# Two transformer blocks on one core: a table load and a weight split moved at the first block's attentions, decays' middles moved under a projection, and norms turned through two PSUM pools

## The reference, cut to what matters

```python
def first_block(x, ...):                       # 2 layers
    for i in range(2):
        h = rms_norm(x, ln_attn_g[i])
        dq, dk, dv, mq, mk, mv = split(h @ w_in[i])       # 6 x 512 columns
        # each head of dq, dk, mq, mk is rms-normed over its 64 columns
        y_diff = softmax(dq dk + bias)[0] - lam * softmax(...)[1]  @ dv, rms-normed per head
        y_moba = softmax(mq mk + bias) @ mv
        x = x + concat(y_diff, y_moba) @ w_out[i]
        x = x + conv_ffn(rms_norm(x, ln_ffn_g[i]), w_up[i], conv_w[i], conv_b[i], w_down[i])

def second_block(h_lat, ctx, ...):             # 2 layers, latent and context stream
    modulate = lambda h, gain, shift, scale: rms_norm(h, gain) * (1 + scale) + shift
    # layer 0: an RWKV-7 scan in both directions over 8 heads, whose decays are
    #   w = exp(-exp(-softplus(-w_raw) - 0.5)), and a windowed attention of 8 heads with a sink
    # layer 1: a neighbourhood attention and a global attention, latent stream alone
    h = h + gate * rms_norm(mixer(modulate(h)) @ w_out)     # both streams in layer 0
    f = square(relu(modulate(h) @ w_ff1)) @ w_ff2
    h = h + gate * rms_norm(f)
```

## Time and profile before

| | us |
|---|---|
| median of 3 runs | 2012.1 (2010.51 to 2012.96) |
| the profiled execution, its own time | 2011.27 |
| its span in the profile | 2009.2 |
| PE busy in the span | 1901.4 (95%) |
| DVE busy | 1122.7 (56%) |
| ACT busy | 867.5 (43%) |
| POOL busy | 211.4 (11%) |

### The profile page before, as it was taken

The page is one execution under the profiler, slowest core; times in us unless marked ns, Lnnn a source line. Parts: engine busy times, 40 slices in busy tenths (PEclk is TensorE's granted clock), DMA queues, the critical chain, the costliest instruction groups (busy, mean ns, idle before and its releaser), DMA issues. The chain is left out here.

```text
span 2009.2 us, 36599 instructions
## 1 busy us (share of the span) xinstructions
PE 1901.4 (95%) x15600; PEld 1591.5 (79%) x15600; DVE 1122.7 (56%) x1758; ACT 867.5 (43%) x1559; POOL 211.4 (11%) x249
## 2 busy tenths in 40 slices
PE   7989999998999999989999998999999989988998
PEld 5758998775899888756898987888877787678987
DVE  6655774565566564475557665544444646436643
ACT  5465663445456542455322335322232344545532
POOL 1100221110022100102112211000000101000000
PEclk9989999998999999999999998999999999988999
DMA  7666665466666542343000042333332224024653
GB/s 266 232 228 210 189 189 169 167 230 210 208 170 187 180 138 62 111 152 122 25 4 4 3 148 63 117 95 112 98 99 90 84 66 145 1 64 128 187 189 126
DMA packets 219352, 264.52 MB, mean 132 GB/s; under 512 B 14214, under 2 KB 153782, under 8 KB 214711
## 3 DMA queue, kind: packets, MB, share of 16 engines
q1 hardware_dynamic: 218603, 261.36, 40.8%
q10 hardware_dynamic: 588, 0.82, 0.1%
HBM read 261.07 MB, written 1.09 MB: 130 GB/s over the span
## 5 line engine op out<-in xcount | busy, mean ns | idle before, releaser
L403 PE MATMUL acc<-rounded,rounded 128*128 128x512 f32 (+1 forms) x2552 | 880.3, 345 | 27.8 <-DVE rounded L675 12.9
L404 PE MATMUL acc<-rounded,rounded 128*128 128x512 f32 (+1 forms) x2552 | 871.2, 341 | 0.0
L405 PE MATMUL acc<-rounded,rounded 128*128 128x512 f32 (+1 forms) x2552 | 870.8, 341 | 0.0
L387 DVE TENSOR_TENSOR rounded<-arena,rounded 128x2048 fp32r<-128x2048 f32 (+1 forms) x194 | 434.4, 2242 | 298.7 <-ACT rounded L376 298.6
L403 PEld LDWEIGHTS acc<-rounded,rounded 128*128 128x128 f32 x2552 | 484.7, 190 | 100.1 <-issue 24.2
L404 PEld LDWEIGHTS acc<-rounded,rounded 128*128 128x128 f32 x2552 | 484.8, 190 | 60.4 <-issue 1.9
L405 PEld LDWEIGHTS acc<-rounded,rounded 128*128 128x128 f32 x2552 | 484.1, 190 | 60.3
L376 ACT ACTIVATE rounded<-arena 128x2048 fp32r<-128x2048 f32 (+1 forms) x194 | 363.0, 1874 | 361.2 <-PE acc L405 319.6
L1523 DVE SCALAR_TENSOR_TENSOR arena<-acc,pcol,arena 128x254 f32<-128x254 f32 (+1 forms) x176 | 76.8, 478 | 52.3 <-ACT arena L1504 50.7
L851 PEld LDWEIGHTS sc<-arena 128*128 128x128 f32 x592 | 73.2, 196 | 37.1 <-ACT arena L975 23.2
L2109 PE MATMUL sc<-arena 64*64 64x64 f32 x2560 | 95.4, 224 | 6.8 <-DVE arena L2259 5.9
(11 more groups left out here) (258 smaller groups left out, 1634.7 us busy)
## 6 DMA issues: line engine op xcount, KB each, us to landing
arena<-in_w_ff SPq DMA_DIRECT2D x64, 1024.0 KB, 5.3
arena<-in_w_ada SPq DMA_DIRECT2D x48, 1024.0 KB, 5.2
arena<-in_w_up SPq DMA_DIRECT2D x88, 512.0 KB, 4.8
arena<-in_w_in SPq DMA_DIRECT2D x24, 1024.0 KB, 5.2
arena<-in_w_down SPq DMA_DIRECT2D x20, 1024.0 KB, 5.1
arena<-in_w_out SPq DMA_DIRECT2D x16, 1024.0 KB, 5.0
arena<-in_w_in_even SPq DMA_DIRECT2D x9, 1024.0 KB, 5.4
arena<-in_w_in_odd SPq DMA_DIRECT2D x8, 1024.0 KB, 5.2
```

What stands on the lines that cost most here:

```text
L387: dve.tensor_tensor(r32(w), w, r32(high_slot(c)[:, 0:size(c)]), ALU.subtract).then_inc(split_made, 1)
L403: pe.matmul(ps, ah, bh, start=first, stop=False)
L404: pe.matmul(ps, ah, bl, start=False, stop=False)
L405: return pe.matmul(ps, al, bh, start=False, stop=last)
```

## The change

It has five edits.

- **First block's layers, end of the projection.** In the last of the six column blocks neither ACT nor DVE splits a weight chunk. The chunk in question, the third of the out-projection, is split by the call that already stood behind the attention and the turning of its result. ACT computes one exponential of a constant before the last two value copies, so that its function table is loaded there.
- **Latent attention.** `decays_dve` for both directions is called in `projB_dve`, behind the sums and ahead of the queries' rotation. The attention's hook no longer calls it.
- **Norms before the feed-forwards.** The second tile of each of them is turned into the two sc banks. DVE does line 670 for both tiles first and then line 675 for both (`norm_lows_by_two`).
- **Layer 0's feed-forward norms.** Context lows now stand ahead of the last latent tile's residual update, ACT squares the second latent tile behind the context highs, and PE turns the latent tiles one weight column earlier each.
- **Out-projection of the second block's layer 1.** DVE's low part of the second chunk of `ff1_1` is made behind the norm rather than between the two halves of the residual. SP's wait for a norm's turn names the new bank.

```diff
-        TWO_POOLS = {("attn", 1): "acc", ("ffn", 0): "acc", ("ffn", 1): "acc", ("mix", 1, 1): "sc", ("mix", 1, 0): "sc"}
+        TWO_POOLS = {("attn", 1): "acc", ("ffn", 0): "acc", ("ffn", 1): "acc", ("mix", 1, 1): "sc", ("mix", 1, 0): "sc",
+                     ("ff", 0, 1): "sc", ("ff", 0, 0): "sc", ("ff", 1, 0): "sc"}
...
+        def norm_shifted(dve, norm, tt):
+            key, src, ready, gain, shift, dst = norm
+            f, hi, lo, cols = norm_quarter(norm, tt, 0)
+            ps = filled(dve, *f)
+            for k, (kt, c) in enumerate(cols):
+                ins = dve.tensor_scalar(lo[:, k, :], ps[:, c], gain(kt), shift(kt), ALU.mult, ALU.add)
+            ins.then_inc(drain(*f), 1)
...
+        def norm_lows_by_two(dve, norm):
+            for tt in range(TT):
+                norm_shifted(dve, norm, tt)
+            for tt in range(TT):
+                for half in range(2):
+                    norm_low(dve, norm, tt, half, shifted=True)
...
+        def load_exp_table(act):
+            act.wait_ge(half_set, 1)
+            act.activation(exp_probe[:, :], half[:, 0:1], ACT.Exp)
...
         def qkv_act(act, l):
             for cb in range(6):
                 ahead_act(act, g + 2 * cb + HIGH)
+                if cb == 5:
+                    load_exp_table(act)
...
-                ahead_act(act, g + 2 * cb + 1 + HIGH)
+                if cb < 5:
+                    ahead_act(act, g + 2 * cb + 1 + HIGH)
...
         def qkv_dve(dve, l):
...
-                ahead_dve(dve, g + 2 * cb + 1 + HIGH)
+                if cb < 5:
+                    ahead_dve(dve, g + 2 * cb + 1 + HIGH)
...
         def projB_dve(dve):
...
+            for d in range(2):
+                decays_dve(dve, d)
             for tt in range(TT):
                 wait_drained(dve, "acc", acc_at["projB"] + 4 + tt)
                 rope(dve, q_tok(TT + tt), 8, tt, rope_t, roped, TT + tt + 1)
...
-                if u < 2:
-                    decays_dve(dve, u)
-                else:
+                if u >= 2:
                     kd_dve(dve, *divmod(u - 2, 4))
...
+                self.split_limit = chunk_at["ff1_1"] if key == "mix1" else len(chunks)
...
                             if following and t >= 2:
                                 norm_scale(dve, following, t - 2)
+                            if latent and t == n - 1:
+                                norm_lows_by_two(dve, following)
+                                norm_scale(dve, latent, 0)
...
-                    feat_gemm_by_stream(pe, ("ff1", 0), acc_at[("ff1", 0)], ET, lambda s: ("ff", 0, s), {2: [0], 3: [1]})
+                    feat_gemm_by_stream(pe, ("ff1", 0), acc_at[("ff1", 0)], ET, lambda s: ("ff", 0, s), {1: [0], 2: [1]})
...
+            norm_square(act, ff_lat, 0)
+            norm_highs(act, ff_ctx)
+            norm_square(act, ff_lat, 1)
+            norm_highs(act, ff_lat)
```

More of the change, by code:

```diff
@@ L661, in norm_high, with norm_low @@
                 ins.then_inc(norm_high_set, 1)
-        def norm_low(dve, norm, tt, half):
+        def norm_shifted(dve, norm, tt):
[5 more added lines that the diff above has]
+            ins.then_inc(drain(*f), 1)
+        def norm_low(dve, norm, tt, half, shifted=False):
             key, src, ready, gain, shift, dst = norm
             f, hi, lo, cols = norm_quarter(norm, tt, half)
-            if shift and half == 0:
-                ps = filled(dve, *f)
-                for k, (kt, c) in enumerate(cols):
-                    ins = dve.tensor_scalar(lo[:, k, :], ps[:, c], gain(kt), shift(kt), ALU.mult, ALU.add)
-                ins.then_inc(drain(*f), 1)
+            if shift and half == 0 and not shifted:
+                norm_shifted(dve, norm, tt)
             dve.wait_ge(norm_high_set, 2 * norm_tile(key, tt) + half + 1)
@@ L1006, in first_and_second_block @@
         sub_gain = stats(DEPTH)
+        exp_probe = stats(1)
         def param_dmas(eng, groups, landed, part=slice(None)):
@@ L2534, in squared, with vector @@
                 dve.wait_ge(post_squared, 2 * self.tiles_before + self.order.index((hf, t)) + 1)
-            def vector(self, dve, following):
+            def vector(self, dve, following, latent=None):
                 n = len(self.tiles)
@@ L2554, in keep_product @@
                             self.update(dve, t)
-                tok_walk(dve, ahead_dve, self.product, self.kts, 2, keep_product, last=False)
+                tok_walk(dve, lambda dve, g: ahead_dve(dve, min(g, self.split_limit)), self.product, self.kts, 2, keep_product, last=False)
+                if latent:
+                    norm_scale(dve, latent, 1)
+                    norm_lows_by_two(dve, latent)
             def add_round(self, dve, key, first):
@@ L2788, in near_dma @@
             if qt == 1 and i == 0:
-                sp.wait_ge(tr_full, tr_at[("norm", ("ff", 0, 0))] + 4)
+                norm_turned(sp, ("ff", 0, 0), 1)
                 sp.dma_start(gain_row[:, 0, :], I["d_q_gain_2"].partition_broadcast(P)).then_inc(gains_landed, 16)
@@ L3155, in _ @@
             rwkv_out_act(act)
-            mix0.scalar(act, mod_norms(0, 1)[0])
-            norm_scalar(act, ("ff1", 0), *mod_norms(0, 1), squared=1)
+            ff_ctx, ff_lat = mod_norms(0, 1)
+            mix0.scalar(act, ff_ctx)
+            norm_square(act, ff_lat, 0)
+            norm_highs(act, ff_ctx)
+            norm_square(act, ff_lat, 1)
+            norm_highs(act, ff_lat)
+            ahead_act(act, chunk_at[("ff1", 0)] + HIGH - 1)
             ff0_scalar(act, ff0, mod_norms(1, 0)[0])
@@ L3273, in _ @@
             rwkv_out_dve(dve)
-            mix0.vector(dve, mod_norms(0, 1)[0])
-            norm_dve(dve, *mod_norms(0, 1), scaled=1)
+            mix0.vector(dve, *mod_norms(0, 1))
             ahead_dve(dve, chunk_at[("ff1", 0)] + HIGH - 1)
@@ L3284, in _ @@
             mix1.vector(dve, None)
-            norm_dve(dve, *mod_norms(1, 1))
+            for tt in range(TT):
+                norm_scale(dve, mod_norms(1, 1)[0], tt)
+            norm_lows_by_two(dve, mod_norms(1, 1)[0])
             ahead_dve(dve, chunk_at["ff1_1"] + HIGH - 1)
```

## The result

The changed kernel took 2003.28 us in the median of 20 runs (1995.94 to 2017.9), beside 2015.74 (2010.51 to 2025.19) for 20 runs of the kernel before on the same chip. The ratio is 0.994, with a 95% interval of 0.9924 to 0.9956: 12 us faster, give or take 3. Both kernels spread by 15 to 22 us from run to run, far more than the three runs that the prediction had to go by. So the two profiles must be compared place by place, not by their ends.

A forecast was written before the change was run, and what follows sets the result against it. PE, busy 1901.4 of 2009.2 us, was taken as the bound, with gains only where it idles or is clocked low. 1.6 + 3.25 + 1.05 + 2.9 + 3.1 + 0.9 = 12.8 us off 2012.1 gave 1999.3, range 1994.5 to 2004.

The forecast's parts named there:

- the forecast's own case: The whole change gains as summed, forecast 1999.3 us; chance 0.65, range 1996 to 2002 us.
- Layer 0's attention, 1.6 us: At its start, without DVE's split ahead of the bias tiles, the first bias addition comes 1.6 us earlier.
- Layer 1's attention, 3.25 + 1.05 us: At its start, PE's wait for the first exponential shrinks by 3.25 us; 1.05 us more from the clock.
- the clock term: Layer 1's attention: low clock behind PE's 3.51 us idle goes with that wait, 1.05 us, ends 0 and 1.1.
- Latent attention, 2.9 us: PE's wait for the first reciprocal, behind decay work on DVE, goes: 2.9 us.
- Layer 0's feed-forward norm, 3.1 us: Ahead of layer 0's feed-forward, the new order lets PE start at 1226.4 in place of 1229.57: 3.1 us.
- The clock's cost: Behind the idle time at layer 0's feed-forward norm, the low clock costs 2.2 us again, since 4 us idle stay.
- Last norm, 0.9 us: Ahead of the last feed-forward, earlier second tile gives 0.7 us and DVE's split some 0.2: 0.9 in all.
- Deferred split and moved decays at nothing: Split behind the attention's turning and decays in DVE's earlier idle time: each priced at 0 us.
- the first (a new wait in place of the old): At the three larger gains, another wait replaces one removed: 2002.4 us, or 2003.3 if both norms' gains go; chance 0.17.
- The second, the clock's own way: Clock falls stay in layer 1's attention and two more come: 2003.4 us, chance 0.10; good side 1996.5 us.

The follow-up runs named there:

- the two kernels with fillers there: Changed kernel with unread products in norm waits and waits around the out-projections and last block, 1998.0 us; the same plus unit 12's attention wait filled, 1994.83 us.
- The parts alone: Kernel before with only the weight split deferred, ratio 0.9996; only the decays moved, 0.9959; only the norms' edits and the last output's held-back split, 0.9976.
- The equal code with unequal low stretches: Changed kernel with attention and decay edits undone, 2012.05 us; up to layer 0's norm its instructions are those of the kernel before.
- the filled wait: Unit 12's wait of 1.72 us in the first block's attentions, filled with two unread products on top of the kernel with other filled waits: 1994.83 us.
- the filled kernel before: Kernel before with unread products in PE's waits at layer 0's feed-forward norm and the last norm: 2015.62 us, ratio 0.9998.

## Why the prediction was right, and where its terms were not

The forecast of 1999.3 us lies 4 below the median and inside the range; taken as a gain, 12.8 us against 12.5 +- 1.2 (difference of the means). The absolute miss is mostly the base: three runs gave 2012.1 for the kernel before, twenty gave 2015.74. For the same reason 2003.28 lies above 1996 to 2002, the range of the forecast's own case, and inside the stated one only because that reached over the rivals. Part of the agreement in the gain is chance, because terms erred in both directions. I checked them over all profiles that have or lack an edit, stretch by stretch.

- *Layer 0's attention, 1.6 us.* The local 1.8 came. From start to out-projection, though, seven profiles with the old split took 58.0 us in the mean (56.9 to 59.1) and five with the new one 57.5 (55.6 to 58.3; the two kernels with fillers there are left out). About 0.5 us is left. All seven profiles with the new split have a low clock somewhere between 100 and 112, of those with the old one two of seven; that the earlier start brings it is likely from this count, but not shown.
- *Layer 1's attention, 3.25 + 1.05 us.* 55.0 (53.4 to 57.6, seven) against 50.8 (50.1 to 51.2, four with the load's move too): 4.2 us. The size was right. The reason given for the clock term was not: the low stretch came again, 2 us later. Some of it went elsewhere: over the whole attention the low clock held for 14 to 27 us (mean 20) in the seven and for 11 to 18 (mean 15) in the four.
- *Latent attention, 2.9 us.* Too small. It measured 4.6: more low clock stands behind the wait than without it, and the sum had priced only the idle time. The pattern stood in the earlier trace rows for layer 1, and I didn't carry it over. This is the term that was mis-sized most.
- *Layer 0's feed-forward norm, 3.1 us.* 385.6 us from the last gate to the first product behind the last block's first wait in four profiles of the old order, 382.4 in five of the new: 3.2. The clock's cost did stay, as said.
- *Last norm, 0.9 us.* The first product comes 0.86 us earlier. To the program's end it is 195.9 against 195.6 us, so 0.3.
- *Deferred split and moved decays at nothing.* Right: the first out-projection product waits 1.53 us as before, and DVE stands idle 4.61 us behind the decays.

The measured terms make 0.5 + 4.2 + 4.6 + 3.2 + 0.3 = 12.8 us. The parts alone, in means against before, are 1.4 (split), 6.7 (decays) and 4.4 us (norms), together 12.5 for the whole's 12.5: they add up within their errors of 1.2 to 1.4 each. Taken out of the whole, the decays were worth 3.3 +- 1.6 and the attention part 2.5 +- 2.8, so the single sizes stay loose by a few microseconds.

Of the rivals, the first (a new wait in place of the old) did not occur. The second, the clock's own way, did in the one profiled execution: it gave back 11 of 12 us there. Its place was not one fall or two, but the attentions and the last block: from the product behind the last block's first wait to its last gate, a stretch in which PE's work is the same in all, it took 202.3 to 212.2 us over twelve profiles, and in the pair 202.3 before and 209.4 after, 7 of the 11 us. The two profiles spent nearly the same time at the low clock (103 us before, 105 after). It lay elsewhere: before, much of it beside PE's waits, after, under PE's work. PE's windows over the same 47 products, before and after:

```profile
1711.71:1717.43 5.72, 5.72 (x47) 0.99 0.00 0
```

```profile
1707.50:1716.95 9.45, 9.45 (x47) 0.58 0.00 0
```

PE is busy throughout both, and the low clock costs 3.7 us.

Over 183 runs of eleven kernels, each run's time against the time that its granted clock says it spent low (2 x (1 - clock) x time), within each kernel, gives 0.42 us per microsecond at the low clock, with a correlation of 0.85; the rest scatters by 2.3 us in place of 4.4. By that count the changed kernel's 29 runs spent 102 us low in the mean and those of before 109. The Trainium skill ("TensorE: Matmul & The Clock Gate", section "What's actually happening") has the monitor run free of the kernel. The equal code with unequal low stretches agrees with that, but the filled wait points to the other half: whether there was a fall between 124 and 152 hung on what the kernel did there.

## What to carry to other kernels

Before pricing an idle time of TensorE by its own length, read the granted clock behind it: here 2.9 us of wait cost 4.6. Not every wait has a low stretch behind it: in the profile before, those of 1.71, 2.49 and 2.64 us at 1614, 1624 and 1638 have none. If a wait with a low stretch can't be shortened, try filling it with products into a bank that is claimed next and overwritten, sized to end just before the wait does; fillers that outlast it give part of the gain back. Compare profiles of such a kernel by local distances, and its versions by many runs, since one execution can differ by 20 us.

## What was not expected of the hardware

A microsecond at the low clock doesn't cost the same everywhere. By the granted clock of the runs the filled kernel before spent 88 us low in the mean, 21 less than before, and was only 1.8 +- 1.6 us faster: much of what its fillers took away had lain ahead of the products, beside PE's waits (in the profile before, the low clock held from 1223.7 to 1233.9 and the first product came at 1229.57). Under PE's unbroken work 8.0 us low cost 3.7. A table load of 1.28 us let the next activation start 1.29 us after its own start. And the scatter between runs of one kernel, which is 15 to 22 us here over 20 runs, was 3 to 7 us in the two kernels with the most waits filled (1996.5 to 1999.1 and 1990.3 to 1997.0), of which there are only 6 and 5 runs.
